# A third buffer for the state-space input, and one gated multiplication moved inside a pooling

## The chip, the cores and the metric

The kernel runs on one core of one Trainium2 chip. The metric is the device time of a whole execution in microseconds (us), as the median of the timed runs.

## The reference, cut to what matters

One layer of a decoder with 1024 tokens and 1024 channels, all float32. Two mixers run side by side on the normalised input h:

```
h = rmsnorm(x) * (1 + scale) + shift
u_pool, z_pool, u_ssm, z_ssm, g_pool, g_ssm = split(h @ w_in)        # six parts of 1024 columns
# mixer A: trailing means over 2, 4, 8, 16 tokens (one window per 256 channels), minus the token
pooled  = trailing_mean(u_pool) - u_pool
y_pool  = (pooled @ pool_w per group) * pool_scale * silu(z_pool)
# mixer B: 64 groups of 16 channels, each with 64 complex states
s[t]    = abar * s[t-1] + bbar * u_ssm[t];   y = Re(C s) + D u_ssm
y       = gelu(y);  y_ssm = y * sigmoid(y @ glu_w + glu_b) * silu(z_ssm)
merged  = sigmoid(g_pool) * (y_pool @ w_branch_pool) + sigmoid(g_ssm) * (y_ssm @ w_branch_ssm)
out     = x + gate * rmsnorm(merged @ w_out)
```

## The kernel before, in words

Each large product is split in three passes of TensorE over a high and a low half of both operands (`x = hi + lo`), 128 output channels at a time ("a job": 48 matmuls of 128x128 by 512 columns). The kernel goes through stages: the norm, eight gate products, then pairs of input products (L2018) with the preparation of the state-space matrices, then **eight turns** m = 0 to 7 (PE's loop at L2132), then the branch, GLU and output products.

In turn m TensorE does, in this order: the product `("up", m)` that makes 128 channels of `u_pool` (line 1937, shared by all products); `part_b(m)` (L2090), 8 small products of the matrices `win` with the state-space input `u_in`; in even turns from 2 on two pooling products `("pp", m-2)` and `("pp", m-1)` (L2121); `part_c(m-1)` (L2099), 16 small products of `taps` with `u_in` of the turn before and of `wout` with the states `sq`; and, in turns 0, 4 and 7, one more input product (`FILL`, for example `("zp", 6)`).

Within a turn VectorE (DVE, loop at L1781) takes the pooling of turn m (`pooling`, L1735: one, two, three or four levels of adding a shifted copy, the tiles `pu`, `pa`, `pb`, then a fix of the first tokens with the small tile `pfix`); in even turns two times `yp_out` (L1760, recorded at L1770), which multiplies a finished pooling product with `silu(z)` in place and releases its PSUM bank; then the split of the next weights (L1398), the rotation, the eight scans, and the rotation back that makes `sq`. PSUM holds products in two alternating banks, `ps0` and `ps1`: `("pp", 4)` and `("up", 7)` share one, so product `("up", 7)` starts only when `yp_out(4)` has been done (`begin`, L1941).

ScalarE (ACT) copies the finished products out of PSUM, makes the high halves, applies the activations and stores `y` by DMAs of its own queue.

SyncE (SP) issues the loads one after another, in the order that is written at L893 to L922. A wait there holds back everything behind it. `u_in` has two buffers: `u_in[m % 2]`. `load_u(b)` (L854) is 8 DMAs of 64 KB in rows of 512 bytes, `load_taps` (L863) another 8, `load_win`, `load_wout` and `load_w` one DMA of 512 KB each. In turn m SP waits for `part_b(m)`, asks for `win` of turn m+1, waits for `part_c(m-1)` (`y_done`), and then asks for `u_in` of turn m+1, for `wout` and `taps` of turn m, for a tile of weights, and for the tables of turn m+2 (four DMAs of 256 KB). TensorE waits for the 8 parts of `u_in` in `part_b` (L2093).

Of the kernel before, what the change touches and what calls it, by code (L numbers as in the profile page):

```python
# [32 lines left out]
P = 128  # L33
D = 1024
KT = D // P
SEQ = 1024
CH = 8
NC = SEQ // CH
HALF = 512
G = 64  # L40
SG = 16
NS = 64
GB = P // SG
# [5 lines left out]
TILE = 4096  # L49
# [96 lines left out]
class Steps:  # L146
# [5 lines left out]
    def did(self, ins):  # L152
        ins.then_inc(self.sem, 1)
        self.k += 1
# [10 lines left out]
def build(nc, x, c_d, cols_d, consts_d, a_re_d, a_im_d, log_dt_d, bc_d, w_ada_d, wstream_d, pool_d, w_out_d, out):  # L165
    ctx = ExitStack()
    with ctx:
        def sem(name):
            return ctx.enter_context(nc.semaphore(name))
# [5 lines left out]
        cur = [-(-nc.sbuf_base // 64) * 64]  # L175
# [31 lines left out]
        rt = [new(f"rt{s}", [P, SEQ]) for s in range(2)]  # L207
        diag = at("diag", [P, CH, P], rt_at)
        a_at = cur[0]
        b_at, c_at = a_at + 8 * TILE, a_at + 16 * TILE  # L210
        cur[0] = a_at + 24 * TILE


        def hb(q, k):
# [44 lines left out]
        def ssm(name, shape, dt=F32):  # L259
            t = at(name, shape, p1[0], dt)  # L260
            p1[0] += nbytes(shape)
            return t
# [24 lines left out]
        win = ssm("win", [P, GB, P])  # L287
        u_in = [ssm("u_in0", [P, GB, NC])]
# [2 lines left out]
        wout = ssm("wout", [P, GB, CH, SG])  # L291
        taps = ssm("taps", [P, GB, CH, SG])
        p1[0] = a_at
        u_in.append(ssm("u_in1", [P, GB, NC]))
        st = ssm("st", [P, GB, NC])
        sw = ssm("sw", [P, GB, NC])
        sq = ssm("sq", [P, GB, NC])
# [12 lines left out]
        zp_t += [t[:, :, :].rearrange("p g c -> p (g c)") for t in (cos_pa, sin_pa)]  # L310
        zp_t += [vta[:, :, :, :].rearrange("p g t h -> p (g t h)"), pu[:, :, :].rearrange("p t c -> p (t c)")[:, 0:SEQ]]
        zs_last = zp_t[6]
        pfix = ssm("pfix", [P, CH, 2])
        assert p1[0] <= c_at, p1[0]

        cols = new("cols", [P, 56])
        consts = new("consts", [P, 232])
# [20 lines left out]
        sign = consts[:, 128:129]  # L338
        inv_n = consts[:, 149:213].rearrange("p (g t c) -> p g t c", t=CH, c=2)
        dmask = consts[:, 213:229]  # L340

        psa = psum("psa")
        ps = [psum("ps0"), psum("ps1"), psa]
        psb = psum("psb")
# [38 lines left out]
        def two(name):  # L383
            return [sem(name + "0"), sem(name + "1")]
# [33 lines left out]
                                                        sem("sin_stored"))  # L418

        win_in, wout_in, taps_in, tables_in, u_loaded = (sem("win_in"), sem("wout_in"), sem("taps_in"),  # L420
                                                         two("tables_in"), two("u_loaded"))
        pads_ready, taps_zero = sem("pads_ready"), sem("taps_zero")
        x_done, swapped, x_taken = sem("x_done"), sem("swapped"), sem("x_taken")
        z_ready, z_used, sq_ready = sem("z_ready"), sem("z_used"), sem("sq_ready")
# [279 lines left out]
        def _(sp):  # L704

            def load_w(p):

                if p >= 2:
                    sp.wait_ge(raw_free[p % 2], p // 2)
                sp.dma_start(raw[p % 2][:, :, :], wstream_d[HOST.index(USES[p])]).then_inc(raw_in[p % 2], 16)  # L710
# [143 lines left out]
            def load_u(b):  # L854

                src = u_d[b].rearrange("(g h) (t c) -> t h g c", h=SG, t=CH)
                for t in range(CH):
                    sp.dma_start(u_in[b % 2][SG * t:SG * t + SG, :, :], src[t]).then_inc(u_loaded[b % 2], 16)

            def load_wout(b):  # L860
                sp.dma_start(wout[:, :, :, :].rearrange("p g t h -> p (g t h)"), wout_d[b]).then_inc(wout_in, 16)
# [6 lines left out]
            def load_tables(b):  # L868

                src = slice(NS * (b % 2), NS * (b % 2) + NS)  # L870
                for dst, table in ((cos_t[b % 2], cos_d[b // 2]), (sin_t[b % 2], sin_d[b // 2])):
                    for r in range(2):
                        sp.dma_start(dst[NS * r:NS * r + NS, :, :].rearrange("p g c -> p (g c)"), table[src]).then_inc(tables_in[b % 2], 16)
# [16 lines left out]
            load_taps(0)  # L890
            load_u(1)
            load_tables(1)
            for m in range(KT):  # L893
                i, last = m // 2, m == KT - 1
                sp.wait_ge(x_done, m + 1)
                if not last:
                    load_win(m + 1)
                if m:
                    sp.wait_ge(y_done, m)
                    if not last:  # L900
                        load_u(m + 1)
                    load_wout(m)
                    load_taps(m)
                load_w(USE["up", m] + 4)
                if m == 2:
                    sp.wait_ge(pair_stored[(NP - 3) % 2], 32 * ((NP - 1) // 2))
                    for n in (4, 5):
                        sp.dma_start(zp_t[n], zp_d[n]).then_inc(zp_in, 16)
                if m == 1:
                    sp.wait_ge(job_out[slot(("zs", 7))], evicted(("zs", 7)))  # L910
                    sp.dma_start(zs_d[7], zs_last).then_inc(zs_stored, 16)
                if m + 2 < KT:
                    sp.wait_ge(cos_stored, 16 * (m // 2 + 2))
                    sp.wait_ge(sin_stored, 16 * (m // 2 + 2))
                    sp.wait_ge(sq_ready, m + 1)
                    load_tables(m + 2)
                if m % 2 and not last:
                    sp.wait_ge(pw_ready, i + 1)
                    load_pw(i + 1)
                for u in FILL.get(m, ()):  # L920
                    if u != ("zp", 7):
                        load_w(USE[u] + 4)  # L922
# [16 lines left out]
            p = USE["bp", 0]  # L939
# [448 lines left out]
        def _(dve):  # L1388
# [343 lines left out]
            def pooled_in(m):  # L1732
                return pb if m // 2 % 2 == 0 else pa

            def pooling(m):  # L1735

                i = m // 2
                dve.wait_ge(job_out[slot(("up", m))], evicted(("up", m)))
                if m:
                    dve.wait_ge(pool_lo_done, m)  # L1740
                s, o = pu, pa
                for l in range(i + 1):
                    d = 1 << l
                    if d < CH:
                        did(tt(o[:, d:, 1:], s[:, d:, 1:], s[:, 0:CH - d, 1:], ALU.add))  # L1745
                    do(tt(o[:, 0:d, 1:], s[:, 0:d, 1:], s[:, CH - d:, 0:NC], ALU.add))
                    s, o = o, (pb if o is pa else pa)
                did(stt(o[:, :, 1:], s[:, :, 1:], 1.0 / WINDOWS[i], pu[:, :, 1:], ALU.mult, ALU.subtract))

                first = lambda z: z[:, :, 1:3]  # L1750
                do(tt(pfix[:, :, :], first(s), inv_n[:, i, :, :], ALU.mult))
                tt(first(o), pfix[:, :, :], first(pu), ALU.subtract).then_inc(pooled, 1)
# [7 lines left out]
            def yp_out(n):  # L1760

                dve.wait_ge(mm_done, JOB["pp", n] + 1)
                if n < 4:
                    dve.wait_ge(func_done, 2 * (n // 2 + 1 + NP - 6))
                    dve.wait_ge(c21_done, NP - 1 + n // 2)
                elif n < 6:
                    dve.wait_ge(zp_in, 32)
                else:
                    dve.wait_ge(job_out[slot(("zp", n))], evicted(("zp", n)))
                stt(zp_t[n], ps[slot(("pp", n))][:, :], pscale[:, n:n + 1], zp_t[n],  # L1770
                    ALU.mult, ALU.mult).then_inc(job_out[slot(("pp", n))], 1)
# [8 lines left out]

            for m in range(KT):  # L1781
                i, even = m // 2, m % 2 == 0
                pooling(m)
                if even and m:
                    yp_out(m - 2)
                    yp_out(m - 1)
                split_lo(USE["up", m] + 2)
                if m == KT - 1:
                    pool_low(m)
                    in_low(0)  # L1790
                    in_low(1)
                rotate_in(m)
                if m < KT - 1:
                    scans(m)
                    pool_low(m)
                if even:
                    pool_weights_low(i)
                for u in FILL.get(m, ()):
                    if u != ("zp", 7):
                        split_lo(USE[u] + 2)  # L1800
                if m < KT - 1:
                    rotate_out(m)
# [91 lines left out]
            for t in range(CH):  # L1894
                one = slice(t, t + 1)
                last = t == CH - 1
# [26 lines left out]
        def _(pe):  # L1923
            mm = nc.tensor.matmul
# [165 lines left out]
            def part_b(m):  # L2090

                pe.wait_ge(win_in, 16 * m + 16)
                pe.wait_ge(u_loaded[m % 2], 16 * CH * (m // 2) + 16 * CH)  # L2093
                pe.wait_ge(x_taken, m)
                for g in range(GB):
                    last = mm(psa[:, g * P:g * P + P], win[:, g, :], u_in[m % 2][:, g, :], start=True, stop=True)  # L2096
                last.then_inc(x_done, 1)

            def part_c(m):  # L2099

                pe.wait_ge(sq_ready, m + 1)
                pe.wait_ge(wout_in, 16 * m + 16)
                pe.wait_ge(taps_in, 16 * CH * m + 16 * CH)
                pe.wait_ge(y_taken, m)
                if m == 0:
                    pe.wait_ge(c21_done, NP)
                for g in range(GB):
                    mm(psb[:, g * P:g * P + P], taps[:, g, :, :].rearrange("p r h -> p (r h)"), u_in[m % 2][:, g, :],  # L2108
                       start=True, stop=False)
                    last = mm(psb[:, g * P:g * P + P], wout[:, g, :, :].rearrange("p r h -> p (r h)"), sq[:, g, :],  # L2110
                              start=False, stop=True)
                last.then_inc(y_done, 1)
# [144 lines left out]
```

## Time and profile before

| | |
|---|---|
| median of 3 timed runs | 959.12 us (956.46, 959.12, 959.93) |
| profiled execution | 955.21 us |
| its span, first to last instruction | 953.4 us |
| TensorE matmul busy | 930.4 us, 98% of the span |
| TensorE weight load busy | 782.2 us, 82% |
| VectorE / ScalarE / GpSimd busy | 639.8 / 349.9 / 45.3 us |
| granted TensorE clock, mean | 0.999 of full speed |
| bytes moved by DMA | 164.60 MB, mean 173 GB/s |

The profile is one execution with every instruction's start and duration. The chain of work that ended last is TensorE's for 94% of the span, so a change can save at most what TensorE stands still, unless it takes work from it. TensorE's own work is the same before and after this change.

### The profile page before, as it was taken

What the parts mean: (1) busy time and instruction counts of PE and PEld (TensorE: products, weight loads), DVE (VectorE), ACT (ScalarE), POOL (GpSimd) and SP (SyncE); (2) the same over time, 40 slices, a digit from 0 to 9 for tenths busy, and PEclk for the clock granted to TensorE, in tenths of its full rate; (3) what the DMA queues carried; (4) which work ended last, traced back from release to release, by engine and by line L of the source; (5) the groups of instructions that cost most, each with busy time, mean ns of one, the idle gap of its engine ahead of it and who ended that gap; (6) DMA issues with size and microseconds to landing.
All of it is one profiled execution on the core that took longest, in us unless ns stands there. A gap on an engine that the chain in (4) does not pass through costs nothing.

```text
span 953.4 us, 11609 instructions
## 1 busy us (share of the span) xinstructions
PE 930.4 (98%) x4408; PEld 782.2 (82%) x4408; DVE 639.8 (67%) x916; ACT 349.9 (37%) x455; POOL 45.3 (5%) x82
## 2 busy tenths in 40 slices
PE   3999999999999999999999999999999999999997
PEld 3888888888888888888888888888888888888885
DVE  5988899877788887437988798665344444455232
ACT  5751353334444444434443446341022221223111
POOL 0019800000000000000000000000000000000000
PEclk9999999999999999999999999999999999999999
DMA  9843355445555344556798572696543258322222
GB/s 348 302 151 124 124 200 168 155 159 195 173 191 203 142 179 148 192 135 181 210 256 208 161 201 58 189 353 238 184 164 109 89 223 216 134 89 89 89 88 89
DMA packets 95719, 164.60 MB, mean 173 GB/s; under 512 B 38576, under 2 KB 55088, under 8 KB 95664
## 3 DMA queue, kind: packets, MB, share of 16 engines
q1 hardware_dynamic: 86304, 159.40, 50.7%
q10 hardware_dynamic: 9360, 4.46, 1.8%
q8 instruction: 35, 0.57, 0.2%
q14 instruction: 20, 0.16, 0.1%
HBM read 116.64 MB, written 47.19 MB: 172 GB/s over the span
## 4 chain that ended last, share of the span: by engine, by line
PE 94%; DVE 3%; ACT 1%; DMA 1%; issue 0%; SPq 0%; DVEq 0%; ACTq 0%
PE ps L1937 48%; PE ps L2057 20%; PE ps L2165 9%; PE psb L2057 8%; PE ps L2121 2%; PE psa L2015 1%; PE psa L2096 1%; PE psa L1937 1%; PE psb L2110 1%; PE psb L2108 1%; PE psb L1965 1%; DMA x_tok<-in_x 1%; PE psb L2015 0%; DVE pa L1745 0%; PE ps L1965 0%
## 5 line engine op out<-in xcount | busy, mean ns | idle before, releaser
L1937 PE MATMUL ps<-bop,w_hi 128*128 128x512 f32 x1120 | 300.8, 391 | 0.9 <-DVE cos_pa L1770 0.8
L1937 PEld LDWEIGHTS ps<-bop,w_hi 128*128 128x128 f32 x1120 | 209.4, 188 | 43.9 <-issue 1.3
L1937 PE MATMUL ps<-bop,w_lo 128*128 128x512 f32 x560 | 172.6, 390 | 0.0
L1937 PEld LDWEIGHTS ps<-bop,w_lo 128*128 128x128 f32 x560 | 105.2, 188 | 21.8
L1398 DVE TENSOR_TENSOR w_lo<-raw,w_hi 128x1024 fp32r<-128x1024 f32 x43 | 53.1, 1235 | 48.3 <-ACT w_hi L1017 48.1
L2057 PE MATMUL ps<-bop,r_hi 128*128 128x512 f32 x272 | 83.8, 390 | 0.0
L1017 ACT ACTIVATE w_hi<-raw 128x1024 fp32r<-128x1024 f32 x43 | 45.3, 1054 | 74.1 <-PE ps L1937 62.0
L2057 PEld LDWEIGHTS ps<-bop,r_hi 128*128 128x128 f32 x272 | 51.1, 188 | 10.5
L2057 PE MATMUL ps<-t_hi,r_hi 128*128 128x512 f32 x140 | 55.1, 394 | 0.0
L2057 PE MATMUL ps<-t_hi,r_lo 128*128 128x512 f32 x140 | 54.6, 390 | 0.0
L2057 PE MATMUL ps<-t_lo,r_hi 128*128 128x512 f32 x140 | 54.6, 390 | 0.0
L2057 PE MATMUL ps<-bop,r_lo 128*128 128x512 f32 x136 | 53.0, 390 | 0.0
L2165 PE MATMUL ps<-wo_lo,y_hi 128*128 128x512 f32 x128 | 49.9, 390 | 0.0
L2165 PE MATMUL ps<-wo_hi,y_hi 128*128 128x512 f32 x128 | 49.9, 390 | 0.0
L2165 PE MATMUL ps<-wo_hi,y_lo 128*128 128x512 f32 x128 | 49.9, 389 | 0.0
L1630 DVE TENSOR_TENSOR r_lo<-r_f,r_hi 128x512 fp32r<-128x512 f32 x56 | 37.3, 688 | 10.2 <-ACT r_hi L1130 10.2
L1858 DVE SCALAR_TENSOR_TENSOR y_raw<-gt,y_raw 128x1024 f32<-128x1024 f32 x8 | 9.8, 1226 | 47.9 <-ACT gt L1085 47.9
L1937 PE MATMUL ps<-y_lo,w_hi 128*128 128x512 f32 x128 | 39.5, 390 | 0.0
L1937 PE MATMUL ps<-y_hi,w_hi 128*128 128x512 f32 x128 | 39.5, 390 | 0.0
L1937 PE MATMUL ps<-y_hi,w_lo 128*128 128x512 f32 x128 | 39.4, 390 | 0.0
L1130 ACT ACTIVATE r_hi<-r_f 128x512 fp32r<-128x512 f32 x56 | 32.3, 624 | 16.3 <-DVE r_f L1610 12.6
L1903 DVE TENSOR_SCALAR stat<-stat 128x1 f32<-128x1 f32 x7 | 1.1, 154 | 49.3 <-ACT squares L1377 49.3
(318 smaller groups left out, 1605.6 us busy)
## 6 DMA issues: line engine op xcount, KB each, us to landing
raw<-in_wstream SPq DMA_DIRECT2D x52, 512.0 KB, 4.4
pair_raw<-in_wstream SPq DMA_DIRECT2D x26, 512.0 KB, 4.2
ada<-in_w_ada SPq DMA_DIRECT2D x16, 512.0 KB, 11.3
x_tok<-in_x SPq DMA_DIRECT2D x8, 512.0 KB, 6.6
gs_d<-gt SPq DMA_DIRECT2D x8, 512.0 KB, 4.9
win_d<-win_new SPq DMA_DIRECT2D x8, 512.0 KB, 2.7
wout_d<-wout_new SPq DMA_DIRECT2D x8, 512.0 KB, 3.8
wout<-wout_d SPq DMA_DIRECT2D x8, 512.0 KB, 5.8
```

What stands on the lines that cost most here:

```text
L1017: fn((wx_hi if p == 2 else w_hi[p % 2])[:, :, :], raw[p % 2][:, :, :], ACT.Copy).then_inc(hi_done, 1)
L1130: fn(r_hi[o // 4][:, o % 4, :].rearrange("p (k m) -> p k m", m=P), src, ACT.Copy).then_inc(pair_hi, 1)
L1398: tt(lo[:, :, :], raw[p % 2][:, :, :], hi[:, :, :].bitcast(F32), ALU.subtract).then_inc(raw_free[p % 2], 1)
L1630: tt(lo, full, hi.bitcast(F32), ALU.subtract).then_inc(pair_lo, 1)
L1858: stt(y_raw[:, n, :], gt[n % 2][:, :], 1.0, y_raw[:, n, :], ALU.add, ALU.mult).then_inc(gated, 1)
L1937: last = mm(ps[slot(u)][:, f * HALF:f * HALF + HALF], a[:, k, :], b(k, f), start=k == order[0] and q == 0, stop=k == order[-1] and q == 2)
L1965: last = mm(xt[k][:, t * P:t * P + P], x_tok[:, t, k * P:k * P + P], diag[:, t, :], start=True, stop=True)
L2015: last = mm(bank[:, at_:at_ + P + SG], vg, eye_c[:, g, :], start=True, stop=True)
L2057: last = mm(bank, a, b, start=k == 0 and q == 0 and not adds, stop=k == 3 and q == 2, skip_group_check=adds)
L2096: last = mm(psa[:, g * P:g * P + P], win[:, g, :], u_in[m % 2][:, g, :], start=True, stop=True)
L2121: last = mm(ps[slot(u)][:, f * HALF:f * HALF + HALF], a[:, 2 * q + k, :], b[:, k, f * HALF:f * HALF + HALF], start=k == 0 and p == 0, stop ...
L2165: ins = mm(ps[slot(("out", t))][:, f * HALF:f * HALF + HALF], a[:, k, t * P:t * P + P], b[:, f * HALF:f * HALF + HALF], start=first and q ...
```

## The change

`u_in` gets a third buffer, with a third semaphore, and the turns use `u_in[m % 3]`. To make room, the small tile `pfix` moves into 16 columns of `consts` that nothing reads, and the region that starts at `c_at` (among others `win`, `u_in0`, `pool_hi`, `pool_lo`, `wout`, `taps`, later `y_lo`) begins 96 bytes later. The tiles behind `u_in1` (`st`, `sw`, `sq`, the tables, the pads) begin 4096 bytes later.

SP asks for `u_in` of turn 2 before the loop. In the turns it asks for `u_in` of turn m+2 (not m+1), and only after `wout`, `taps` and the weights.

In turn 6, whose pooling has four levels, `yp_out(4)` is issued behind the pooling's first level instead of behind the whole pooling.

```
-        b_at, c_at = a_at + 8 * TILE, a_at + 16 * TILE
-        cur[0] = a_at + 24 * TILE
+        b_at, c_at = a_at + 8 * TILE, a_at + 16 * TILE + 96
+        cur[0] = c_at + 8 * TILE
...
-        u_in.append(ssm("u_in1", [P, GB, NC]))
+        u_in += [ssm("u_in1", [P, GB, NC]), ssm("u_in2", [P, GB, NC])]
...
-        pfix = ssm("pfix", [P, CH, 2])
+        pfix = consts[:, 129:145].rearrange("p (t c) -> p t c", c=2)
...
-                    sp.dma_start(u_in[b % 2][SG * t:SG * t + SG, :, :], src[t]).then_inc(u_loaded[b % 2], 16)
+                    sp.dma_start(u_in[b % 3][SG * t:SG * t + SG, :, :], src[t]).then_inc(u_loaded[b % 3], 16)
...
             load_u(1)
             load_tables(1)
+            load_u(2)
             for m in range(KT):
                 i, last = m // 2, m == KT - 1
                 sp.wait_ge(x_done, m + 1)
                 if not last:
                     load_win(m + 1)
                 if m:
                     sp.wait_ge(y_done, m)
-                    if not last:
-                        load_u(m + 1)
                     load_wout(m)
                     load_taps(m)
                 load_w(USE["up", m] + 4)
+                if m and m + 2 < KT:
+                    load_u(m + 2)
...
-            def pooling(m):
+            def pooling(m, behind_first=None):
...
                     s, o = o, (pb if o is pa else pa)
+                    if l == 0 and behind_first is not None:
+                        behind_first()
...
-                pooling(m)
+                inside = m == KT - 2
+                pooling(m, (lambda: yp_out(m - 2)) if inside else None)
                 if even and m:
-                    yp_out(m - 2)
+                    if not inside:
+                        yp_out(m - 2)
                     yp_out(m - 1)
...
-                pe.wait_ge(u_loaded[m % 2], 16 * CH * (m // 2) + 16 * CH)
+                pe.wait_ge(u_loaded[m % 3], 16 * CH * (m // 3) + 16 * CH)
```

`part_b` and `part_c` read `u_in[m % 3]` in the same way.

## Rows read from the trace of the kernel before

**Rows 1.** The page: engines' busy us and shares, TensorE's granted clock in tenths.

```profile
PE 930.4 (98%) x4408; PEld 782.2 (82%) x4408; DVE 639.8 (67%) x916; ACT 349.9 (37%) x455; POOL 45.3 (5%) x82
PEclk9999999999999999999999999999999999999999
```

**Rows 2.** Who waited for whom, PE: line, releaser, us in total, times, longest.

```profile
PE psb L1965 <- DVE diag L1425: 15.5, 1, 15.5
PE ps L1937 <- DVE cos_pa L1770: 0.8, 1, 0.8
PE psa L2096 <- issue: 0.4, 1, 0.4
PE ps L1937 <- DVE bop L1446: 0.2, 1, 0.2
```

**Rows 3.** PE in time (start, us, instruction): first product behind part_c(1) to (5).

```profile
452.42 1.17 PE L1937 MATMUL ps<-bop,w_hi 128*128 128x512 f32 x4
...
474.12 1.17 PE L1937 MATMUL ps<-bop,w_hi 128*128 128x512 f32 x4
...
490.38 1.17 PE L1937 MATMUL ps<-bop,w_hi 128*128 128x512 f32 x4
...
512.76 0.94 PE L1937 MATMUL ps<-bop,w_hi 128*128 128x512 f32 x3
...
539.89 1.17 PE L1937 MATMUL ps<-bop,w_hi 128*128 128x512 f32 x4
...
562.61 1.17 PE L1937 MATMUL ps<-bop,w_hi 128*128 128x512 f32 x4 [0.77 <-DVE cos_pa L1770]
```

**Rows 4.** PE in time: part_b(4) and its wait.

```profile
501.94 2.02 PE L2096 MATMUL psa<-u_in,win 128*128 128x128 f32 x16 [0.42 <-issue]
```

**Rows 5.** SP's queue in time, turns 2 and 3 (start, us, issue).

```profile
484.39 0.59 SPq L710 DMA_DIRECT2D raw<-in_wstream  x1
...
488.61 0.58 SPq L852 DMA_DIRECT2D win<-win_d  x1
490.65 3.68 SPq L858 DMA_DIRECT2D u_in<-u_d  x8
```

**Rows 6.** Landing of win and u_in of turn 4; second 495 by engine, clock, DMA share, GB/s.

```profile
win<-win_d SPq DMA_DIRECT2D x1, 512.0 KB, 9.8
```

```profile
L858 SPq DMA_DIRECT2D u_in<-u_d x8: 325/432/452, 490.7 to 493.9; - x8
DMA to landing us min/median/max: 7.1/7.2/8.0
```

```profile
495.00:496.00 1.00, 1.00 (x6) 0.83 (x5) 0.96 (x4) 0.00 (x0) 0.00 (x0) 1.00 1.04 246
```

**Rows 7.** DVE in time, turn 6, and the PE row between its two pooling products.

```profile
555.51 0.29 DVE L1746 TENSOR_TENSOR pa<-pu 128x128 f32<-128x128 f32 x1
...
561.18 1.28 DVE L1770 SCALAR_TENSOR_TENSOR cos_pa<-ps,cols,cos_pa 128x1024 f32<-128x1024 f32 x1
```

```profile
555.39 0.62 PE L2121 MATMUL ps<-pool_hi,pw_hi 128*128 128x512 f32 x2
```

**Rows 8.** SP's queue in time, before turn 1.

```profile
424.71 4.82 SPq L858 DMA_DIRECT2D u_in<-u_d  x8
...
432.03 0.58 SPq L852 DMA_DIRECT2D win<-win_d  x1
```

**Rows 9.** Landing of that win load, the DMAs from 440 (last columns), part_b(1) on PE.

```profile
win<-win_d SPq DMA_DIRECT2D x1, 512.0 KB, 6.6
```

```profile
440.00:441.00 1.00, 1.00 (x6) 0.83 (x5) 1.00 (x2) 0.00 (x0) 0.00 (x0) 1.00 0.00 0
```

```profile
447.14 1.94 PE L2096 MATMUL psa<-u_in,win 128*128 128x128 f32 x16
```

**Rows 10.** ACT and DVE in time, turn 7.

```profile
586.54 1.06 ACT L1275 ACTIVATE bop<-gt 128x1024 fp32r<-128x1024 f32 x1 [1.97 <-PE ps L1937]
```

```profile
587.63 1.23 DVE L1779 TENSOR_TENSOR bop<-gt,bop 128x1024 fp32r<-128x1024 f32 x1 [1.80 <-ACT bop L1275]
```

More of the change, by code:

```diff
@@ L420, in build @@
         win_in, wout_in, taps_in, tables_in, u_loaded = (sem("win_in"), sem("wout_in"), sem("taps_in"),
-                                                         two("tables_in"), two("u_loaded"))
+                                                         two("tables_in"), [sem(f"u_loaded{q}") for q in range(3)])
         pads_ready, taps_zero = sem("pads_ready"), sem("taps_zero")
@@ L2092, in part_b @@
                 pe.wait_ge(win_in, 16 * m + 16)
-                pe.wait_ge(u_loaded[m % 2], 16 * CH * (m // 2) + 16 * CH)
+                pe.wait_ge(u_loaded[m % 3], 16 * CH * (m // 3) + 16 * CH)
                 pe.wait_ge(x_taken, m)
                 for g in range(GB):
-                    last = mm(psa[:, g * P:g * P + P], win[:, g, :], u_in[m % 2][:, g, :], start=True, stop=True)
+                    last = mm(psa[:, g * P:g * P + P], win[:, g, :], u_in[m % 3][:, g, :], start=True, stop=True)
                 last.then_inc(x_done, 1)
@@ L2107, in part_c @@
                 for g in range(GB):
-                    mm(psb[:, g * P:g * P + P], taps[:, g, :, :].rearrange("p r h -> p (r h)"), u_in[m % 2][:, g, :],
+                    mm(psb[:, g * P:g * P + P], taps[:, g, :, :].rearrange("p r h -> p (r h)"), u_in[m % 3][:, g, :],
                        start=True, stop=False)
```

## The prediction

> **What bounds the kernel now.** I read the page first: the matmul row is 98% of the span, at a granted clock of nine tenths or more in every slice [rows 1], which is the 2.4 GHz level. The change takes no matmul away. So it can only return time in which TensorE stands still, and the second view, who waited for whom on PE, lists all of that time: 15.5 us once at the head, and 0.8, 0.4 and 0.2 us [rows 2]. The head (first tile transposed behind the norm's first statistics) and the 0.2 us (splitting of h) lie long before the turns and are not touched. What is left, 0.8 us on the releaser `cos_pa` at L1770 and 0.4 us in front of L2096, are the two places of this change: L1770 is `yp_out`, and L2096 is `part_b`, which waits for `u_in` and `win`.
>
> The third view, PE in order of time, gives the true price, since a queue that has run dry also loses the overlap of neighbouring matmuls. I take the start of the product that follows `part_c` as the mark and measure even turns against each other, because they hold the same work (48 product matmuls, 16 records of `part_b`, 24 of pooling, 32 of `part_c`). Turn 2: 474.12 - 452.42 = 21.70 us. Turn 4: 512.76 - 490.38 = 22.38 us. Turn 6: 562.61 - 539.89 = 22.72 us [rows 3]. Turn 2 has no wait. So turn 4 loses 0.68 us (0.42 of idle [rows 4] and 0.26 of lost overlap) and turn 6 loses 1.02 us (0.77 [rows 3] and 0.25). Together 1.70 us, 0.18% of the time. That is the whole prize of the turns.
>
> **The change part by part.**
>
> *The third u buffer.* The wait of 0.42 us at L2096 has "issue" as its releaser, so I look for the DMA. SP asked for `win` of turn 4 at 488.61 and for `u_in` of turn 4 from 490.65 on [rows 5]. `win` needed 9.8 us: it was there at 498.4. The last of the 8 parts of `u_in` was issued at 493.9 and the slowest took 8.0 us: 501.9 [rows 6]. `part_b(4)` started at 501.94 [rows 4]. So it was `u_in`. After the change `u_in` of turn 4 is asked for in turn 2, behind `wout`, `taps` and weights: SP's issues in turn 2 are the same number in another order, so its last part leaves where `raw` did before, near 485.0 [rows 5]. With even 8.0 us to land it is there at 493, 8 us early. Gain 0.68 us.
>
> What is late next at `part_b(4)` is `win`, at 498.4 against the mark of about 501.5, 3.1 us early. The transfers in front of it on SP's queue are the same in number and bytes as before; only the eight parts of u stand nearer to it. Bounds for its landing: from no change to one u load later, 3.68 us of issue [rows 5], which would make it 502.1 and leave 0.6 us of the stall. I take no change, because the transfers that changed places with u (`wout`, `taps`, `raw`) are as large as it. `wout` and `taps` of a turn are asked for about 4 us sooner, the weights too; none of them is waited for in [rows 2], so that gains nothing. The tables are asked for where they were, since in each turn SP gets to them only after a wait for `sq`. `u_in` of turn m+2 is now behind `load_w`'s wait for a free weight buffer. Behind it on SP stand only the tables and `win` of the next turn, and u itself has a full turn to land.
>
> *The u load ahead of the loop.* This is the one place where the change adds work in front of something. `load_u(2)` puts 8 more issues before `win` of turn 1. They take SP as long as the ones of turn 1 did, 4.82 us, so `win` leaves at 432.03 + 4.82 = 436.85 instead of 432.03 [rows 8]. It needed 6.6 us [rows 9]: 443.5. PE wants it at 447.14 [rows 9]. Bounds for its landing: 443.5, and 436.85 + 9.8 (the longest of `win` [rows 6]) + 4.8 (all of u queued in front) = 451.5. I take 443.5 to 446, because the 16 DMA engines had nothing to do at all from 440 on [rows 9], so there is room for 512 KB more. Cost nothing; with that cover gone up to 451.5 - 447.1 = 4.4 us. The weights behind it slip by the same 4.8 us and are wanted by ACT only once PE has begun `part_b(1)`.
>
> The Trainium skill, page "DMA: Bandwidth & Descriptors", section "Bandwidth", has a transfer of 64 KB run at 138 GB/s, so eight of them would hold the engines for an estimated 3.8 us; section "Queues, rings and completion order" says that each ring takes its descriptors in order. By the two `win` would land near 443.5 + 3.8 = 447.3, a stall of some 0.2 us in turn 1, and the forecast would be 957.6 instead of 957.4. No row here shows those eight loads with nothing behind them.
>
> *The multiplication inside the pooling.* In turn 6 DVE is through the pooling's first level at 555.51 + 0.29 = 555.8 and comes to `yp_out(4)` at 561.18, 1.28 us long [rows 7]. PE had put down the last matmul of the first pooling product by 555.39, where the second begins [rows 7], so the operand is ready at about 555.6. Issued behind the first level, `yp_out(4)` runs from 555.9 to 557.2. PE ends `part_c(5)` at about 561.8 and finds the bank free 4.6 us before. The wait of 1.02 us goes whole. Price: the rest of the pooling of turn 6 ends 1.28 us later, at 562.5. Who waits for it: ACT's high half, which stands behind the gelu of `part_c(5)` that PE ends only at 561.8, so it loses nothing; then the second multiplication, which starts where it did. DVE's sum of work is unchanged. Cost between 0 and 0.1 us on DVE, off PE's path: I take 0.
>
> *The moved addresses.* Nothing in the trace has the operands of TensorE at another offset. Below: no gain has a reason. Above: DVE has the same 1.28 us for `yp_out` whether its tile is `cos_pa`, in the area behind the odd-sized pads, or another. I take 0, and keep 1 us for the range. `pfix` in `consts` costs nothing that a row would show.
>
> *Is the gain kept to the end?* PE runs 1.70 us ahead from turn 7 on. Behind it, ACT and DVE must be able to follow. ACT stood 1.97 us idle until PE released the high half of turn 7, and DVE 1.80 us behind it [rows 10]; both were started by PE's end of product 5, which itself comes 0.68 us sooner. So DVE's pooling chain moves 0.68 and its idle time shrinks from 1.80 to about 0.8 us: it still waits for PE, not the other way. The first branch product starts behind `yp_out(6)`, which DVE reaches through that same chain, and moves with it. After that no row of PE's waits exists to the end [rows 2].
>
> *Sum.* 0.68 + 1.02 = 1.70 us off the profiled execution, 955.21 to 953.5, span 953.4 to 951.7. The timed median lies 3.9 us above the profiled execution; I carry the difference over: 959.12 - 1.70 = 957.4 us.
>
> **The rivals.**
>
> *A. One of the two returns.* The gain of turn 4 or the slack of 0.8 us in turn 7 is eaten by another chain (`win` of turn 4, DVE in turn 7). Worked out: 0.68 to 1.02 us are left, 958.1 to 958.4. For it: the DMA engines are full there (share 1.04 at 495), and the landing times there reach 9.8 us [rows 6]. Against it: the margins of 3.1 and 0.8 us.
>
> *B. The other side: `win` of turn 1 comes late behind `load_u(2)`.* It decides from a landing after 447.1, and makes the kernel slower than before once it is later than 447.1 + 1.7 = 448.8, that is 12.0 us after its issue. At the upper bound of 451.5 the sum is +4.4 - 1.7 = +2.7, 961.8 us. For it: SP's queue is one, and the load is new there. Against it: no `win` took over 9.8 us, and the engines were idle from 440.
>
> *C. The stall on u is larger in the timed runs than in the profiled one.* They are 1.3 to 4.7 us above it. If half of that is u in other turns (it landed with little to spare wherever it was asked for one turn ahead), the change returns another 1 to 2.5 us: 955 to 956.5. For it: turn 4's DMA wait depends on contention, which differs from run to run. Against it: no other turn shows a DMA wait.
>
> *D. It does not do what it says*: nothing moves, 959.1.
>
> **How the numbers follow.** Forecast 0.60, A 0.18, B 0.05, C 0.13, D 0.04. The predicted time is the forecast's, 957.4. The bound of what can be told from no change is 0.5%, 4.8 us: below 954.3 or above 963.9. The prize of 1.7 us does not reach it; only C with a lucky median does (0.08), and on the other side B at its end with unlucky runs (0.02). Within: 0.90. The range takes in that the three runs before lie 3.5 us apart: from 957.4 - 3.6 = 953.8 (C, and the profiled run's own 953.5 nearly) to 960.2 (B in part, or the highest run with 1 us for the addresses).
>
> **What would show it.** Right: PE's waits list neither L1770 nor L2096; turns 4 and 6 measure 21.7 us like turn 2; `yp_out(4)` starts near 555.9 less 0.7; the chain's span is 951.7. Wrong: a wait at L2096 near 447 (B); PE waiting in turn 7 or behind it on `pool_lo` or a bank (A); longer matmuls at L2108 to L2121 (addresses).

## The result: slower by half a percent

The changed kernel takes 963.22 us (median of 8 runs, 962.50 to 963.97). The kernel before took 959.34 us in its 8 runs beside it (954.89 to 960.95). The ratio is 1.0050 (95% interval 1.0032 to 1.0069; it is worked out from all the runs, the quotient of the two medians is 1.0040): slower, outside my range of 953.8 to 960.2, and just under the 963.9 beyond which I had put 2 in 100. The only rival that made the kernel slower was B, with 0.05, and its cause is not the one found here. The profiled span is 960.7 us, against 953.4.

The first view, who waited for whom on PE in the changed kernel, says that the change did what it was made for. Neither `cos_pa` nor `psa` is left:

```profile
PE psb L1973 <- DVE diag L1428: 14.9, 1, 14.9
PE ps L1945 <- DVE bop L1449: 0.5, 1, 0.5
```

PE in order of time, the six marks of [rows 3] (L1945 is the old L1937), so rows 1 to 2, 3 to 4 and 5 to 6 span turns 2, 4 and 6:

```profile
456.72 1.17 PE L1945 MATMUL ps<-bop,w_hi 128*128 128x512 f32 x4
...
478.46 0.70 PE L1945 MATMUL ps<-bop,w_hi 128*128 128x512 f32 x2
...
494.75 0.93 PE L1945 MATMUL ps<-bop,w_hi 128*128 128x512 f32 x3
...
516.49 1.17 PE L1945 MATMUL ps<-bop,w_hi 128*128 128x512 f32 x4
...
543.65 1.17 PE L1945 MATMUL ps<-bop,w_hi 128*128 128x512 f32 x4
...
565.39 1.17 PE L1945 MATMUL ps<-bop,w_hi 128*128 128x512 f32 x4
```

The three even turns measure 21.74, 21.74 and 21.74 us, where [rows 3] had 21.70, 22.38 and 22.72. The gain is there, 1.6 us. DVE in turn 6 has `yp_out(4)` behind the first level, and the second one at its old place in the row ([rows 7] had the first at 561.18):

```profile
559.26 0.29 DVE L1749 TENSOR_TENSOR pa<-pu 128x128 f32<-128x128 f32 x1
559.58 1.28 DVE L1775 SCALAR_TENSOR_TENSOR cos_pa<-ps,cols,cos_pa 128x1024 f32<-128x1024 f32 x1
...
566.13 1.28 DVE L1775 SCALAR_TENSOR_TENSOR sin_pa<-ps,cols,sin_pa 128x1024 f32<-128x1024 f32 x1
```

So the loss is elsewhere, and not a wait. The chain that ended last (start, us, what, count) of the kernel before, and under it that of the changed kernel, with four pieces each: the first and the last half product of the pair stage, 1068 matmuls of the first branch, the GLU and the second branch in one piece, and the output products:

```profile
130.03 2.72 PE ps L2057 x12
...
412.86 2.72 PE ps L2057 x12
...
618.09 242.09 PE ps L1937 x1068
860.18 87.05 PE ps L2165 x384
```

```profile
129.81 2.81 PE ps L2065 x12
...
417.01 2.81 PE ps L2065 x12
...
620.97 244.24 PE ps L1945 x1068
865.21 89.32 PE ps L2173 x384
```

The same matmuls in the same number take longer, with no idle time between them: twelve of a half product 2.81 us and not 2.72, the 384 of the output 89.32 and not 87.05. The pair stage went from 285.55 (415.58 - 130.03) to 290.01 us (419.82 - 129.81): +4.46. The long piece: +2.15. The output: +2.27. Together 8.9 us, in stages that the third buffer does not reach. The granted clock is at the 2.4 GHz level in both (mean 0.999 and 0.998). What these stages have in common is that they read an operand from the region at `c_at` (`r_hi0` and `r_lo0` as weights, `y_lo` as moving operand in the GLU, `m_lo` as weights in the output), which now begins 96 bytes later. The last 288 matmuls of the stage of the gate products read nothing there and take 65.28 us in both. The third gate product, whose weights `wx_hi` lie there, is 0.2 us longer.

### The profile page after: what moved, and what is told of

Read it like the earlier page. It is cut to its first block, busy times and chain, and to the rows that moved or that the text cites. A ratio compares the mean times of both kernels' runs of the same rounds, so it can differ in the third digit from the quotient of the medians.

```text
span 960.7 us, 11609 instructions
## 1 busy us (share of the span) xinstructions
PE 939.1 (98%) x4408; PEld 781.9 (81%) x4408; DVE 639.7 (67%) x916; ACT 349.8 (36%) x455; POOL 45.3 (5%) x82
## 3 DMA queue, kind: packets, MB, share of 16 engines
q10 hardware_dynamic: 9360, 4.46, 1.9%
## 4 chain that ended last, share of the span: by engine, by line
PE 97%; DMA 1%; SPq 1%; ACT 0%; DVE 0%; issue 0%; DVEq 0%
PE ps L1945 49%; PE ps L2065 20%; PE ps L2173 9%; PE psb L2065 8%; PE ps L2129 2%; PE psb L2118 1%; PE psb L2116 1%; PE psa L2104 1%; PE psa L2023 1%; DMA raw<-in_wstream 1%; PE psa L1945 1%; PE psb L2023 0%; PE psb L1973 0%; SPq L740 0%; PE psa L1973 0%; DVE bop L1449 0%
## 5 line engine op out<-in xcount | busy, mean ns | idle before, releaser
L1945 PE MATMUL ps<-bop,w_hi 128*128 128x512 f32 x1120 | 300.8, 390 | 0.5 <-DVE bop L1449 0.5
L1945 PEld LDWEIGHTS ps<-bop,w_hi 128*128 128x128 f32 x1120 | 209.3, 188 | 43.5 <-issue 0.6
L1945 PE MATMUL ps<-bop,w_lo 128*128 128x512 f32 x560 | 172.5, 389 | 0.0
L1945 PEld LDWEIGHTS ps<-bop,w_lo 128*128 128x128 f32 x560 | 105.1, 188 | 22.1
L1945 PE MATMUL ps<-y_lo,w_hi 128*128 128x512 f32 x128 | 40.4, 397 | 0.0
L1945 PE MATMUL ps<-y_hi,w_lo 128*128 128x512 f32 x128 | 40.3, 395 | 0.0
L1945 PE MATMUL ps<-y_hi,w_hi 128*128 128x512 f32 x128 | 39.7, 391 | 0.0
```

Of the source, the lines that this page charges most:

```text
L1945: last = mm(ps[slot(u)][:, f * HALF:f * HALF + HALF], a[:, k, :], b(k, f), start=k == order[0] and q == 0, stop=k == order[-1] and q == 2)
```

## The experiments

I held the theory that the addresses cost it (L: a start that is no multiple of 64 bytes) against the new order of the loads (Q), the tiles moved by 4096 bytes or `pfix` (T), and the distance between a matmul's operands (D). In these comparisons the kernel before has medians of 956.8 to 957.5 us, over 17 to 35 runs. Each ratio is worked out from all runs of both kernels, so it is not the quotient of two medians, and differences of a few tenths of a per cent rest on its interval.

**e1_shift96.** The kernel before with nothing but the shift. It moves the region, and with it all that lies behind it: the small tiles and the pooling weights `pw_hi` and `pw_lo`.

```
-        b_at, c_at = a_at + 8 * TILE, a_at + 16 * TILE
-        cur[0] = a_at + 24 * TILE
+        b_at, c_at = a_at + 8 * TILE, a_at + 16 * TILE + 96
+        cur[0] = c_at + 8 * TILE
```

> The kernel before with one edit: the region at c_at, and all small tiles behind it, begin 96 bytes later. Two u buffers, all orders as before. Theory L (a TensorE operand whose start is 32 bytes past a multiple of 64 makes its matmuls longer): the pair stage about 4.5 us, the GLU and branch products 2.1 us and the output products 2.3 us longer, none of the turns' gain: 959.3 + 8 to 9 = 967.5 to 968.5 us, both waits of the turns still there. Rival Q (the new order of the u loads costs it): 959.3 us, within 1 us, and output products of 87.05 us. Rival T (the tiles moved by 4096 bytes, or pfix inside consts, cost it): 959.3 us too.

Measured: 969.09 us (6 runs), ratio 1.011 (1.0083 to 1.0137). The long piece and the output, in the chain:

```profile
627.82 244.24 PE ps L1937 x1068
872.06 89.32 PE ps L2165 x384
```

They are the changed kernel's to the hundredth. The addresses cost it; Q and T are dead. The time is even higher than expected. The profile shows a reason in turn 4. PE in order of time, and the busy time by engine there (columns: PE, PEld, DVE, ACT, POOL busy, then granted clock, DMA share, GB/s):

```profile
509.93 3.55 PE L2096 MATMUL psa<-u_in,win 128*128 128x128 f32 x16 [3.60 <-issue]
```

```profile
506.00:510.00 4.00, 0.40 (x3) 0.10 (x1) 3.93 (x6) 1.97 (x2) 0.00 (x0) 1.00 1.20 226
510.00:512.00 2.00, 2.00 (x11) 2.00 (x11) 1.97 (x4) 0.00 (x0) 0.00 (x0) 0.54 1.04 240
```

The wait for `u_in`, 0.42 us in the one profile that I had [rows 4], is 3.60 us here, and behind it TensorE runs at about half its clock (0.54, the 1.2 GHz level), so that `part_b(4)` takes 3.55 us and not 2.02. The part of `u_in` that came last took 11.2 us to land, not 8.0.

**e2_aligned.** The changed kernel with 128 bytes.

```
-        b_at, c_at = a_at + 8 * TILE, a_at + 16 * TILE + 96
+        b_at, c_at = a_at + 8 * TILE, a_at + 16 * TILE + 128
-        pfix = consts[:, 129:145].rearrange(...)
+        pfix = mod_acc[:, :].rearrange(...)          # consts: 212 columns, not 232
```

> The changed kernel, with the region at c_at 128 bytes later and not 96, so that it and everything behind it start at a multiple of 64 again (pfix lies in mod_acc, and consts loses the 20 columns that nothing reads). Theory L: the output products take 87.05 us again, the pair stage and the GLU lose their surplus, the turns keep their 1.7 us: span 951.7 us, 957.4 us timed. Rivals Q and T: still 963 us. Rival D (it is the distance between weights and moving operand, not the absolute place): still 963 us, since every distance has changed by 128 bytes.

Measured: 961.09 us (12 runs), ratio 1.0028 (1.0012 to 1.0043). Two us better than with 96 bytes, not six. Its chain has the long piece at 243.41 and the output at 88.77 us. L as I had put it is refuted: a start at a multiple of 64 does not bring the lost time back.

**e3_shift64 and e4_shift32.** As e1, with 64 and 32 bytes.

```
-        b_at, c_at = a_at + 8 * TILE, a_at + 16 * TILE
+        b_at, c_at = a_at + 8 * TILE, a_at + 16 * TILE + 64      # e4: + 32
```

> The kernel before with the region 64 bytes later. Theory L with a multiple of 64: as the kernel before, 959.3 us, output products 87.05 us. If a multiple of 128 is what counts: as with 96 bytes, 967 to 968 us. Rival D: something else than 959.3.

> The kernel before with the region 32 bytes later. Theory L with a multiple of 64: the same loss as with 96 bytes, 967.5 to 968.5 us. If the loss grows with the distance from a boundary of 128 or 256: clearly different from the loss with 96 bytes. Rivals Q and T: 959.3 us.

Measured: 966.44 (ratio 1.0083, 1.0053 to 1.0112) and 967.10 us (1.0087, 1.0054 to 1.012), 4 runs each. Both are slow, so a start at a multiple of 64 is no cure in the kernel before either. That left D.

**e5_gap1024 and e6_gap256.** The changed kernel, with the region at a distance of 1024 and of 256 bytes from its old place. The 96 bytes that the pads need and some small tiles fill the gap, so nothing else grows.

```
-        b_at, c_at = a_at + 8 * TILE, a_at + 16 * TILE + 96
+        b_at, c_at = a_at + 8 * TILE, a_at + 16 * TILE + 256     # e5: + 1024
+        # mod_acc, g_col, s_col, gate_col (e5: consts) begin at a_at + 16 * TILE + 96
```

> The changed kernel, but the region at c_at begins 1024 bytes later than in the kernel before (the 96 bytes of the pads and the tile consts lie in front of it). Theory D (it is the place of an operand of a matmul relative to those of the matmuls beside it, counted within some block of bytes: in the kernel before all large tiles start at whole steps of 4096 bytes from each other): if the block is 1024 or a divisor of it, the pair stage takes 285.3 us, GLU 86.8 and output 86.8 us as in the kernel before, and the third buffer keeps the turns at 192.9 us: span 952 us, 954 us timed. If the block is larger: 955 to 963 us. Theory L64 (a start that is no multiple of 64) is dead already by the shift of 64 bytes.

> The same with 256 bytes (the pads' 96 and four small tiles in front). Theory D with a block of 256 bytes: 954 us, as with 1024. With a larger block: the surplus of the aligned kernel (6.4 us over three stages at 128 bytes) or another one in its place, 957 to 963 us.

Measured: 954.61 us (11 runs, ratio 0.9959, 0.9940 to 0.9977) and 954.25 us (12 runs, 953.66 to 955.07, ratio 0.9961, 0.9947 to 0.9975). Both beat the kernel before, by 0.4%. The chain of e6 is back at the old lengths, with the third buffer in:

```profile
616.77 242.09 PE ps L1948 x1068
858.87 87.05 PE ps L2176 x384
```

**e7_base64.** The kernel before, with all of SBUF's tiles 64 bytes later.

```
-        cur = [-(-nc.sbuf_base // 64) * 64]
+        cur = [-(-nc.sbuf_base // 64) * 64 + 64]
```

> The kernel before with every tile in SBUF 64 bytes later, so that all distances are kept. Theory D: stages as in the kernel before (pairs 285.3, GLU 86.8, output 86.8 us), 957 to 959 us. If the absolute place counts (a multiple of 128 plus nothing): every product is longer, 975 us or more.

Measured: 959.18 us (10 runs, ratio 1.0007, 0.9988 to 1.0027). The chain and, below, PE's row of `part_b(4)`:

```profile
625.08 242.09 PE ps L1937 x1068
867.17 87.05 PE ps L2165 x384
```

```profile
506.27 3.75 PE L2096 MATMUL psa<-u_in,win 128*128 128x128 f32 x16 [4.15 <-issue]
```

The same 64 bytes that cost 1.7 us in the output products in e3 cost nothing if every tile moves with them. It is the distance. And the wait in turn 4 is 4.15 us in this profile, where the matmuls are as fast as before, so a long wait does not need longer matmuls.

**e8_behind_bop64.** `bop`, the moving operand of most products, keeps its place, and everything behind it moves.

```
         ada = at("ada", b_shape, bop_at)
+        cur[0] += 64
         raw_at = cur[0]
```

> The kernel before with bop left in place and every tile behind it 64 bytes later. So weights in w_hi and w_lo now stand 64 bytes off against the moving operand bop, which in the kernel before they did not. Theory D: the gate products (65.5 us) and branch products (87.3 us) now lengthen by 1 to 2 us each, while the GLU products (y and w both behind bop) stay at 86.8. If only the region at c_at is special: 65.5 and 87.3 us as before.

Measured: 975.95 us (2 runs, ratio 1.0186, 1.0148 to 1.0225). The 288 matmuls of the gate products, from the chain of e8 and, for comparison, of the kernel before:

```profile
66.58 67.20 PE ps L1938 x288
```

```profile
64.75 65.28 PE ps L1937 x288
```

Now the gate products are longer, by 1.92 us, and the GLU, whose two operands both lie behind `bop`, stays at 86.8 us. The region at `c_at` is not special. The stages of all layouts side by side, in us, each from the start of its first matmul to the start of its own last one (so they are some tenths shorter than the pieces of the chain):

| kernel | distance of the region at c_at | pairs | GLU | output |
|---|---|---|---|---|
| before | 0 | 285.33 | 86.81 | 86.81 |
| e4 | 32 | 289.04 | 88.51 | 89.36 |
| e3 | 64 | 289.38 | 88.09 | 88.50 |
| changed, e1 | 96 | 289.78 | 88.94 | 89.07 |
| e2 | 128 | 288.76 | 88.08 | 88.51 |
| e6 | 256 | 285.20 | 86.81 | 86.81 |
| e5 | 1024 | 285.20 | 86.81 | 86.81 |
| e7 | 0, all tiles + 64 | 285.35 | 86.81 | 86.81 |
| e8 | all behind bop + 64 | 288.83 | 86.86 | 88.52 |

Two more readings of these traces narrow down what "distance" means. First, in the GLU of the changed kernel only `y_lo` lies in the moved region. Here are its three kinds of matmul (moving operand, weights) in the window from 690 to 770 us, by the mean duration (the last but one number, in ns), first in the kernel before and then in the changed kernel:

```profile
L1937 PE MATMUL ps<-y_hi,w_lo 128*128 128x512 f32 x118 | 36.5, 390 | 0.0
L1937 PE MATMUL ps<-y_lo,w_hi 128*128 128x512 f32 x118 | 36.4, 390 | 0.0
L1937 PE MATMUL ps<-y_hi,w_hi 128*128 128x512 f32 x118 | 36.4, 390 | 0.0
```

```profile
L1945 PE MATMUL ps<-y_hi,w_lo 128*128 128x512 f32 x116 | 36.5, 395 | 0.0
L1945 PE MATMUL ps<-y_lo,w_hi 128*128 128x512 f32 x114 | 36.0, 397 | 0.0
L1945 PE MATMUL ps<-y_hi,w_hi 128*128 128x512 f32 x116 | 36.0, 391 | 0.0
```

Those of `y_hi` with `w_lo` are longer too, though neither operand has moved. So it is not only a matmul's own pair that counts: matmuls beside one at a bad distance lengthen with it. Whether that comes through the weights loaded for the next matmul or another way, no run tells.

Second, the gap that e5 and e6 fill moved the pooling weights. `pw_hi` and `pw_lo` lie behind the small tiles. In the kernel before they begin 3840 bytes (15 times 256) past a whole step of 4096 from their moving operand `pool_hi`; in e6 it is 3680 bytes, which is 96 past a multiple of 256, and e5 is 96 past one too. The 24 pooling matmuls of turn 2, in the chain of the kernel before and of e6:

```profile
465.34 5.46 PE ps L2121 x24
```

```profile
465.05 5.62 PE ps L2132 x24
```

That is 0.16 us, 3%, and the four such groups have it each in e5, e6, e9 and e12: about 0.6 us that these kernels still leave. A layout that keeps this distance too was not run. In e2 the distance is 192 past a multiple of 256, and the group takes 5.51 us.

**e9 to e12: what each part brings, and whether the buffer was needed.** e9 is e6 with the multiplication back at its old place.

```
-                inside = m == KT - 2
+                inside = False
```

> The kernel of e6_gap256 (third buffer, region 256 bytes later) with yp_out(4) back behind the whole pooling. Theory: the buffer brings nearly all, the moved multiplication 1.0 us: turns 194.2 us against 193.2, 954.25 + 1.0 = 955.3 us, with the narrow spread of the kernels with the third buffer (1.5 us). Rival: the moved multiplication brings nothing in the timed runs, 954.3 us.

Measured: 955.02 us (12 runs, 954.06 to 955.45, ratio 0.9972, 0.9957 to 0.9986), 0.8 us over e6. The profiles agree: from the pooling products of turn 6 to those behind turn 7 it is 0.85 us more than in e6. PE's waits name the one place:

```profile
PE ps L1948 <- DVE cos_pa L1778: 0.6, 1, 0.6
```

e10 is the kernel before with only the multiplication moved (the two hunks of `pooling` and its call).

> The kernel before with only yp_out(4) moved into the pooling: two u buffers, no address moved. Theory: 1.0 us less than before, with the wide spread of before (955 to 963 us), since the wait for u in turn 4 stays: a median of 956 to 958.5 us. Rival: the third buffer was not needed, 954.3 us.

Measured: 956.61 us (12 runs, 954.92 to 959.54, ratio 0.9994, 0.9978 to 1.0011): nothing that can be told, and the wide spread stays. Its profile has the wait for u in between:

```profile
PE psa L2100 <- issue: 1.4, 1, 1.4
```

e11 is e10 with two buffers and another cure for that wait: the 1 MB of `silu(z)` that SP asks for in turn 2, just ahead of the tables, `win` and u of turn 4, is asked for in turn 4.

```
-                if m == 2:
+                if m == 4:
                     sp.wait_ge(pair_stored[(NP - 3) % 2], 32 * ((NP - 1) // 2))
                     for n in (4, 5):
                         sp.dma_start(zp_t[n], zp_d[n]).then_inc(zp_in, 16)
```

> The kernel before with yp_out(4) moved and the two loads of silu(z) from memory (cos_pa and sin_pa, 512 KB each) asked for in turn 4 and not in turn 2; two u buffers, no address moved. Theory: the u load of turn 4 is late because these 1 MB and four table loads stand in front of it, so it lands 2 to 4 us sooner, the wait in turn 4 goes: 954 to 955 us, narrow spread, as good as e6_gap256 without a third buffer. Rival: the engines are full there with or without them, the wait stays: 956 to 958.5 us.

Measured: 954.12 us (12 runs, 953.23 to 954.74, ratio 0.9966, 0.9949 to 0.9982). The u load of turn 4, by its own rows, against 8.0 us at the most in [rows 6]:

```profile
L858 SPq DMA_DIRECT2D u_in<-u_d x8: 330/432/451, 491.9 to 495.1; - x8
...
DMA to landing us min/median/max: 4.8/5.0/5.4
```

The slowest part lands 2.6 us sooner, and the wait is gone from PE's list. One changed condition, with no byte of SBUF more, does what the third buffer does; the rival, that the engines are too full there in any case, falls.

e12 is e6 with u asked for ahead of `wout` and `taps`.

```
+                    if m + 2 < KT:
+                        load_u(m + 2)
                     load_wout(m)
                     load_taps(m)
                 load_w(USE["up", m] + 4)
-                if m and m + 2 < KT:
-                    load_u(m + 2)
```

> The kernel of e6_gap256, but u of turn m+2 is asked for ahead of wout and taps (as the u load stood in the kernel before), not behind the weights. Theory: with a whole turn to land the place makes no difference: 954.3 us. Rival: taps of turn m, now 4 us later, are late for part_c: a wait at the small products and 955 us or more.

Measured: 954.14 us (10 runs, 953.86 to 956.49, ratio 0.9968, 0.9951 to 0.9986), and no wait for `taps`. With a turn to spare the place in the queue does not matter.

## Why the prediction was wrong, point by point

- **What bounds the kernel** held: PE's own time, and only its waits to win. But I read from it that the change "can only return time in which TensorE stands still". It could also make the matmuls longer, and that is what it did: 8.9 us of longer matmuls against 1.6 us of standstill returned.
- **The moved addresses**: this is the step that failed. I took 0 and kept 1 us. Measured: 4.46 + 2.15 + 2.27 = 8.9 us, and 0.2 us in the product with `wx_hi`. My ground was a row of DVE, whose 1.28 us do not depend on where the tile lies. No row had the operands of TensorE's products of 512 columns at an odd distance: in the kernel before they are whole steps of 4096 bytes apart, or, for the pooling weights, 3840 bytes past one. So I had a bound from the wrong engine, and none from the right one. My sign of being wrong looked in the wrong place as well, at L2108 to L2121 in the turns, where the changed kernel loses 0.04 us per even turn (21.74 against 21.70). The loss sits in the pair stage, the GLU and the output, which the prediction never named. e1 shows the cost alone, e6 its absence.
- **The third u buffer**: the mechanism held (0.68 us in turn 4 in the profiled execution, and all of it came back). For the timed runs the term was mis-sized. The wait is 0.42, 1.4, 2.5 (e8), 3.5 (e3), 3.5 (e4), 3.60 and 4.15 us in the seven profiles of kernels with two buffers and the loads in the old order, and the four longest cost clock on top. I take it for the wide spread of the kernel before (954.0 to 961.9 us over 35 runs). The evidence is indirect, since the only profile of that kernel is of a short run (955.21 us): every run over 958.8 us has a mean granted clock of 0.995 to 0.997 and every one under 957.6 us 0.998 or 0.999, and e11, which differs from e10 only in when the two loads of `silu(z)` are asked for, narrows the spread from 4.6 to 1.5 us. In the changed kernel, e2, e5, e6 and e9, which have no such wait, it is 1.2 to 1.5 us; in e12 it is 2.6, by one run of ten. Rival C, to which I gave 0.13, was right that the stall is larger in the timed runs, but put the surplus in other turns; every profile has it in turn 4. Buffer and moved multiplication together, at a distance of 256 bytes, are worth 957.3 - 954.25 = 3.0 us.
- **The u load ahead of the loop** held: `win` of turn 1 was issued at 441.83, behind the eight, and took 5.6 us, so it was there 4 us before PE's `part_b(1)`. Rival B did not happen. In the lines from SP's queue:

```profile
437.88 3.91 SPq L860 DMA_DIRECT2D u_in<-u_d  x8
441.83 0.43 SPq L854 DMA_DIRECT2D win<-win_d  x1
```

- **By the page "DMA: Bandwidth & Descriptors" of the Trainium skill** (sections "Bandwidth" and "Queues, rings and completion order") `win` would have come an estimated 3.8 us later than without the eight loads. The trace does not agree: it landed in 5.6 us, against 6.6 in [rows 9], so no delay behind them shows. The page's row for 64 KB is for transfers issued from GpSimd, and these went out from SP, which took 3.91 us to issue the eight.
- **The multiplication inside the pooling** held. e9 against e6 has it at 0.8 us, where I had 1.02. e10 alone could not be told from no change.
- **The gain kept to the end** held: no new wait behind turn 7 (A did not happen).
- **The sum**: for the changed kernel -1.4 in the turns, +4.46, +2.15, +2.27 and +0.2 (`wx_hi`), less 0.4 at the head, is +7.3 us, the difference of the spans. In the medians it is +3.9, and the difference fits the long waits, which the changed kernel lost and which the profiled execution of the kernel before happened not to have. One lucky profile hid more than half of what the buffer brings: 0.68 us in it, against 956.8 - 955.0 = 1.8 us in the medians of e9's comparison.

## What to carry to other kernels

When a tile is moved in SBUF, count the move as a change to every matmul that reads it: here a distance from the other operand of 32 to 128 bytes past a multiple of 256 cost 1 to 3% of each such stage, and small tiles in the gap gave it back. Then check every other product whose operands the gap has moved; here the pooling weights were overlooked. Before a buffer is added for a late load, look at what was asked for just ahead of it; here moving one condition did the same. A wait on a DMA that shows 0.4 us in one profile can be ten times that in the next, so read it together with the spread of the runs.

## What the runs showed of the hardware

- The time of the products of 512 columns in fp32r depends on the distance between the SBUF addresses of the weights and the moving operand. Distances of 0, 256 and 1024 bytes (beside whole steps of 4096) were equal to 0.2 us over the pair stage and to 0.01 us over the GLU and the output; 32, 64, 96 and 128 bytes each cost 3.4 to 4.5 us in 285, and 1.3 to 2.6 us in 87. The absolute place cost nothing (e7). Matmuls beside those at such a distance lengthened too (390 to 395 ns in the GLU). Between 128 and 256 bytes only 192 was run, in e2's pooling products: 5.51 us against 5.46. Why, whether a bank or something else, no run here tells. The small products of 128 columns in the turns did not lengthen by more than hundredths.
- The Trainium skill, page "SBUF — State Buffer", section "Who interferes with whom", says that PE never waits on anyone. It speaks there of what other engines do, and no run here tests that. It is no ground to expect one pace in every layout: the same matmuls took up to 3% longer with nothing changed but a distance.
- A standstill of TensorE of 3.60 us was followed by stretches at 0.54 and 0.61 of its clock (e1), and one of 4.15 us by 0.64 and 0.51 (e7). Behind 3.48 us (e3) and 3.52 us (e4) it fell to 0.50 for a stretch as well. Behind 0.42 us [rows 4], 1.39 us (e10) and 2.46 us (e8) the granted clock stayed at 1.00.
